# Quarter-array products in the triangular inverse of the gated delta rule

## The reference, cut to what matters

```
decay = exp(where(i >= j, gc[i] - gc[j], -inf))
lmat  = where(i > j, (k*beta) @ k.T * decay, 0)
tmat  = inverse(lmat + I)                        # unit lower triangular
u     = tmat @ (v * beta);  w = tmat @ (k * beta * exp(gc))
v_new = u - w @ s
o     = q_in @ s + (q @ k.T * decay) @ v_new
s     = s * exp(g_last) + k_out.T @ v_new
```

## Time and the profile before

| | |
|---|---|
| median of 3 runs (lowest, highest) | 3918.93 us (3916.99, 3925.47) |
| the profiled execution's time | 3921.35 us |
| its span, from first to last instruction | 3919.6 us |
| TensorE matmuls | 3528.7 us (90% of the span), 31266 instructions |
| VectorE | 1900.4 us (48%) |
| GpSimd | 1192.2 us (30%) |
| ScalarE | 1067.7 us (27%) |
| chain that ended last | PE 82%, ACT 6%, DVE 6%, issue 4%, DMA 1% |

### The profile page before, as it was taken

One profiled execution on the slowest core, in us unless ns is written; L12 is line 12 of the kernel. 1 busy time (PEld: TensorE's weight loads), 2 busy tenths in 40 slices (PEclk: granted clock), 3 DMA queues, 4 the chain that ended last, 5 costly groups with the idle time before them and its releaser, 6 DMA issues.

```text
span 3919.6 us, 74126 instructions
## 1 busy us (share of the span) xinstructions
PE 3528.7 (90%) x31266; PEld 3368.8 (86%) x31266; DVE 1900.4 (48%) x2402; ACT 1067.7 (27%) x1495; POOL 1192.2 (30%) x562
## 2 busy tenths in 40 slices
PE   8998787799999999989997876777699999999979
PEld 7997787799999999989996445777599999999979
DVE  1563554375454454655412225545447544544564
ACT  2365232242111111241013334222324111111142
POOL 2332532353333333333332000000064333333323
PEclk9999999899999999999998998998899999999989
DMA  3111000221111111112221016121121111111111
GB/s 126 57 52 52 1 0 24 83 65 49 43 43 43 43 43 43 49 56 84 91 72 47 1 43 214 36 43 35 65 99 51 43 43 43 43 43 43 43 44 70
DMA packets 106406, 212.49 MB, mean 54 GB/s; under 512 B 58560, under 2 KB 59840, under 8 KB 105600
## 3 DMA queue, kind: packets, MB, share of 16 engines
q1 hardware_dynamic: 94832, 168.65, 13.8%
q10 hardware_dynamic: 11408, 41.34, 2.7%
HBM read 172.73 MB, written 37.23 MB: 54 GB/s over the span
## 4 chain that ended last, share of the span: by engine, by line
PE 82%; ACT 6%; DVE 6%; issue 4%; DMA 1%; POOL 0%; ACTq 0%; DVEq 0%; SPq 0%; PEldq 0%; POOLq 0%
PE PS L727 56%; PE PS L744 8%; PE PS L1333 6%; PE PS L992 4%; PE PS L1298 1%; PE PS L1397 1%; ACT XH L1654 1%; ACT Y L1655 1%; PE PS L1356 1%; PE PS L1276 1%; DVE XL L2193 1%; PE PS L1273 1%; PE PS L758 0%; PE PS L1258 0%; PE PS L920 0%
## 5 line engine op out<-in xcount | busy, mean ns | idle before, releaser
L727 PE MATMUL PS<-XH,WHI 128*128 128x274 f32 x4320 | 1254.7, 290 | 11.4 <-ACT RN L1549 6.3
L727 PE MATMUL PS<-XL,WHI 128*128 128x274 f32 x4320 | 1254.0, 290 | 0.0
L727 PE MATMUL PS<-XH,WLO 128*128 128x274 f32 x4320 | 1252.0, 290 | 0.0
L843 POOL TENSOR_TENSOR WHI<-RAW,EPS 128x1024 fp32r<-128x1024 f32 x234 | 454.4, 1942 | 2452.5 <-PE PS L727 1417.4
L727 PEld LDWEIGHTS PS<-XH,WHI 128*128 128x128 f32 x4320 | 817.6, 189 | 14.4 <-issue 8.0
L727 PEld LDWEIGHTS PS<-XL,WHI 128*128 128x128 f32 x4320 | 819.2, 190 | 0.0
L727 PEld LDWEIGHTS PS<-XH,WLO 128*128 128x128 f32 x4320 | 818.5, 189 | 0.0
L846 POOL TENSOR_TENSOR WLO<-RAW,WHI 128x1024 fp32r<-128x1024 f32 x234 | 605.0, 2586 | 18.4
L727 PE MATMUL PS<-HH,WHI 128*128 128x274 f32 x1280 | 372.0, 291 | 0.0
L727 PE MATMUL PS<-HH,WLO 128*128 128x274 f32 x1280 | 370.4, 289 | 0.0
L727 PE MATMUL PS<-HL,WHI 128*128 128x274 f32 x1280 | 369.5, 289 | 0.0
(11 more groups left out here) (440 smaller groups left out, 5676.4 us busy)
## 6 DMA issues: line engine op xcount, KB each, us to landing
RAW<-in_units SPq DMA_DIRECT2D x234, 512.0 KB, 3.5
prepared_rows<-PREP SPq DMA_DIRECT2D x8, 1096.0 KB, 5.4
CIN<-prepared_rows SPq DMA_DIRECT2D x17, 512.0 KB, 4.5
c_rows<-DX ACTq DMA_DIRECT2D x14, 548.0 KB, 2.8
RKV<-c_rows SPq DMA_DIRECT2D x4, 1644.0 KB, 11.0
X<-in_x SPq DMA_DIRECT2D x8, 548.0 KB, 9.0
XR<-in_x ACTq DMA_DIRECT2D x8, 548.0 KB, 11.8
bonus_gate_rows<-BG SPq DMA_DIRECT2D x4, 1096.0 KB, 5.0
```

What stands on the lines that cost most here:

```text
L727: last = nc.tensor.matmul(PS[:, 4 * slot + b, 0:width], wt[:, ring, w], r[:, k, b * width:(b + 1) * width], start=n == 0, stop=n == 3 * nk ...
L843: nc.gpsimd.tensor_tensor(WHI[:, s, :], RAW[:, s, :], ZERO.to_broadcast([128, 1024]), ALU.add)\
```

## The change

The matrix of 128 tokens has two diagonal blocks of 64 and one block of 64x64 below them. Levels 0 to 5 never leave the diagonal blocks. After the change they work on buffers of 128 partitions x 4 heads x 64 columns (`TA_B`, `TT_B`, `WW_B`, `LM_B`, `DB_B`), the upper block in the upper half of the partitions and the lower one in the lower half, and every product of them is a `c_heads` group of 16 matmuls of 64x64. The masks of the levels are `BLOCK_LEVEL`, copied once before the loop. VectorE makes the diagonal blocks of `DB` in two halves and, as a new event `below`, the block below them; the transposing product now waits for `below`. Level 6 becomes two products on one quarter, of which one reads the block below in `DB`. Its negated result goes into a quarter of `TT`, and ScalarE copies the two diagonal blocks into `TT` (event `packed`), for which `carry1` now waits. The last quarter of `TT` is set to zero once. `m6` goes away.

```diff
+        BLOCK_LEVEL = at("BLOCK_LEVEL", [128, 6, 64], spare)
+        TT_B = [at("TT_B%d" % p, [128, 4, 64], spare + 1536 + 1024 * p) for p in range(2)]
+        TA_B = [at("TA_B%d" % p, [128, 4, 64], SETS[p][7]) for p in range(2)]
+        DB_B = [at("DB_B%d" % p, [128, 4, 64], SETS[p][7] + 1024) for p in range(2)]
+        WW_B = [at("WW_B%d" % p, [128, 4, 64], SETS[p][9]) for p in range(2)]
+        LM_B = [at("LM_B%d" % p, [128, 4, 64], SETS[p][9] + 1024) for p in range(2)]
...
 # GpSimd
-                    nc.gpsimd.tensor_tensor(LM[p][:, :, :], DB[p][:, :, :], heads_of(level_mask(l)), ALU.mult).then_inc(s, 1)
+                    nc.gpsimd.tensor_tensor(LM_B[p][:, :, :], DB_B[p][:, :, :], pairs_of(BLOCK_LEVEL[:, l, :]), ALU.mult)\
+                        .then_inc(s, 1)
...
-                elif name[0] == "w" and name != "w6":
+                elif name[0] == "w" and int(name[1]) < 5:
...
 # TensorE
                 elif name == "blocks":
-                    pe.wait_ge(gdn_dve[p], G_DVE.at(j, "m0"))
-                    turned(b + 1, LM[p]).then_inc(s, 1)
+                    pe.wait_ge(gdn_dve[p], G_DVE.at(j, "below"))
+                    tiled()
+                    c_heads(stacked(b + 1), LM_B[p], PAIR_ID).then_inc(s, 1)
...
-                    pe.wait_ge(gdn_pool[p], G_POOL.at(j, "m%d" % l))
-                    by_head(b + 1, LM[p], TT[p]).then_inc(s, 1)
+                    if l < 6:
+                        pe.wait_ge(gdn_pool[p], G_POOL.at(j, "m%d" % l))
+                        tiled()
+                        c_heads(stacked(b + 1), LM_B[p], TT_B[p]).then_inc(s, 1)
+                    else:
+
+                        tiled()
+                        for m in range(4):
+                            last = nc.tensor.matmul(stacked(b + 1)[half(0), m, :], DB[p][half(1), m, half(0)], TT_B[p][half(1), m, :],
+                                                    start=True, stop=True)
+                        last.then_inc(s, 1)
...
-                    by_head(b + 2, TA[p], WW[p]).then_inc(s, 1)
+                    tiled()
                     if l < 6:
-                        by_head(b + 3, WW[p], TA[p]).then_inc(s, 1)
+                        c_heads(stacked(b + 2), TA_B[p], WW_B[p]).then_inc(s, 1)
+                        c_heads(stacked(b + 3), WW_B[p], TA_B[p]).then_inc(s, 1)
                     else:
-
+                        for m in range(4):
+                            last = nc.tensor.matmul(stacked(b + 2)[half(0), m, :], TA_B[p][half(0), m, :], WW_B[p][half(0), m, :],
+                                                    start=True, stop=True)
+                        last.then_inc(s, 1)
...
                     pe.wait_ge(gdn_dve[p], G_DVE.at(j, "r"))
+                    pe.wait_ge(gdn_act[p], G_ACT.at(j, "packed"))
                     by_head(b + 1, TT[p], RR[p]).then_inc(s, 1)
...
 # ScalarE
-                    nc.scalar.activation(WW[p][:, :, :], per_head(b + 1), ACT.Copy).then_inc(s, 1)
+                    rows_of = slice(0, 128) if name != "w6" else half(0)
+                    nc.scalar.activation(WW_B[p][rows_of, :, :], stacked(b + 1)[rows_of, :, :], ACT.Copy).then_inc(s, 1)
+                    if name == "w6":
+
+                        act.wait_ge(gdn_dve[p], G_DVE.at(j, "tt5"))
+                        for h in range(2):
+                            last = nc.scalar.activation(TT[p][half(h), :, half(h)], TT_B[p][half(h), :, :], ACT.Copy)
+                        last.then_inc(s, 1)
...
 # VectorE, before the loop
+            for h in range(2):
+                nc.vector.tensor_copy(BLOCK_LEVEL[half(h), :, :],
+                                      small("level", 6 * 128).rearrange("p (l c) -> p l c", l=6)[half(h), :, half(h)])
+            dve.wait_ge(norm_done, 10)
+            for p in range(2):
+                nc.vector.memset(TT[p][half(1), :, half(0)], 0.0)
...
 # VectorE, in the loop
-                    nc.vector.tensor_tensor(DB[p][:, :, :], per_head(b + 1), DB[p][:, :, :], ALU.mult).then_inc(s, 1)
+                    for h in range(2):
+                        last = nc.vector.tensor_tensor(DB_B[p][half(h), :, :], per_head(b + 1)[half(h), :, half(h)],
+                                                       DB[p][half(h), :, half(h)], ALU.mult)
+                    last.then_inc(s, 1)
...
-                    nc.vector.tensor_tensor(LM[p][:, :, :], DB[p][:, :, :], heads_of(level_mask(0)), ALU.mult).then_inc(s, 1)
+                    nc.vector.tensor_tensor(LM_B[p][:, :, :], DB_B[p][:, :, :], pairs_of(BLOCK_LEVEL[:, 0, :]), ALU.mult)\
+                        .then_inc(s, 1)
...
-                    nc.vector.tensor_tensor(TA[p][:, :, :], heads_of(IDENT), LM[p][:, :, :], ALU.subtract).then_inc(s, 1)
+                    nc.vector.tensor_tensor(TA_B[p][:, :, :], pairs_of(PAIR_ID), LM_B[p][:, :, :], ALU.subtract).then_inc(s, 1)
+                    nc.vector.tensor_tensor(DB[p][half(1), :, half(0)], per_head(b + 1)[half(1), :, half(0)],
+                                            DB[p][half(1), :, half(0)], ALU.mult).then_inc(s, 1)
                     dve.wait_ge(gdn_pe[p], G_PE.at(j, "m_turned"))
-                    nc.vector.tensor_tensor(TT[p][:, :, :], heads_of(IDENT), per_head(b + 1), ALU.subtract).then_inc(s, 1)
+                    nc.vector.tensor_tensor(TT_B[p][:, :, :], pairs_of(PAIR_ID), stacked(b + 1), ALU.subtract).then_inc(s, 1)
...
-                    nc.vector.tensor_tensor(TT[p][:, :, :], TT[p][:, :, :], per_head(b + 2), ALU.subtract).then_inc(s, 1)
                     if name != "t6":
+                        nc.vector.tensor_tensor(TT_B[p][:, :, :], TT_B[p][:, :, :], stacked(b + 2), ALU.subtract).then_inc(s, 1)
...
+                        nc.vector.tensor_tensor(TA_B[p][:, :, :], TA_B[p][:, :, :], stacked(b + 3), ALU.subtract).then_inc(s, 1)
                     else:
+                        nc.vector.tensor_scalar(TT[p][half(0), :, half(1)], stacked(b + 2)[half(0), :, :], -1.0, None, ALU.mult)\
+                            .then_inc(s, 1)
```

More of the change, by code:

```diff
@@ L314, in build @@
         KT, QT, VT, DA, DB, EG, LM = [pair(x, n) for n, x in enumerate(("KT", "QT", "VT", "DA", "DB", "EG", "LM"))]
-        TA, TT, WW, VB, KO, RR, VN = [pair(x, 7 + n) for n, x in enumerate(("TA", "TT", "WW", "VB", "KO", "RR", "VN"))]
+        TT, VB, KO, RR, VN = [pair(x, n) for x, n in (("TT", 8), ("VB", 10), ("KO", 11), ("RR", 12), ("VN", 13))]
+        spare = 12 * TILE + 6 * SET
+        BLOCK_LEVEL = at("BLOCK_LEVEL", [128, 6, 64], spare)
[4 more added lines that the diff above has]
+        LM_B = [at("LM_B%d" % p, [128, 4, 64], SETS[p][9] + 1024) for p in range(2)]
         SP, SS = at("SP", [128, 4, 128], AR + 16 * TILE + 14 * SET), at("SS", [128, 4, 128], AR + 16 * TILE + 15 * SET)
@@ L503, in before @@
                 return i * self.count + 1
-        def level_mask(l):
-            return small("level", 128, 128 * l)
         def heads_of(x):
@@ L594, in build @@
                            *[x + str(l) for l in range(1, 7) for x in ("w", "tt", "ta")][:-1], "ks", "v_new", "o", "s")
-        G_DVE = ChunkStages("decayed", "diff", "lower", "m0", "ta0", "t0", "qk",
+        G_DVE = ChunkStages("decayed", "diff", "lower", "m0", "ta0", "below", "t0", "qk",
                             *[x + str(l) for l in range(1, 7) for x in ("tt", "ta")][:-1], "r", "s")
-        G_ACT = ChunkStages("staged", "exps", "ko", "vb", *["w%d" % l for l in range(1, 7)], "v_new", "out")
-        G_POOL = ChunkStages("upper", "m1", "q_in", *["m%d" % l for l in range(2, 7)])
+        G_ACT = ChunkStages("staged", "exps", "ko", "vb", *["w%d" % l for l in range(1, 7)], "packed", "v_new", "out")
+        G_POOL = ChunkStages("upper", "m1", "q_in", *["m%d" % l for l in range(2, 6)])
         C_PE = ChunkStages("vt", "l", "lt", "kg", "bg",
@@ L988, in _, with c_heads, tiled @@
             pe.wait_ge(norm_root, 8)
+            def c_heads(out, lhs, rhs, more=()):
+                terms = [(lhs, rhs)] + list(more)
+                for m in range(4):
+                    for n, (l, r) in enumerate(terms):
+                        for h in range(2):
+                            x = r[half(h), :] if len(r.shape) == 2 else r[half(h), m, :]
+                            last = nc.tensor.matmul(out[half(h), m, :], l[half(h), m, :], x,
+                                                    start=n == 0, stop=n == len(terms) - 1)
+                return last
+            def tiled():
+                pe.sem_inc(c_turn, 1)
             def by_head(bank, lhs, rhs, start=True, stop=True):
@@ L1031, in g_step @@
                     pe.wait_ge(gdn_act[p], G_ACT.at(j, "w%d" % l))
-                    by_head(b + 2, TA[p], WW[p]).then_inc(s, 1)
+                    tiled()
                     if l < 6:
-                        by_head(b + 3, WW[p], TA[p]).then_inc(s, 1)
-                    else:
+                        c_heads(stacked(b + 2), TA_B[p], WW_B[p]).then_inc(s, 1)
```

(6 more changed lines are left out.)

1 line of the change is left out of this document (removed).

## The result

| | median us | runs | profiled span us | clock |
|---|---|---|---|---|
| before | 3920.58 | 7 | 3919.6 | 0.957 |
| after | 3904.36 (3898.26 to 3910.39) | 7 | 3902.6 | 0.951 |

The ratio is 0.9959, 95% interval 0.9948 to 0.9970: 16 us faster, where 38 were forecast, and outside the range on its slow side.

A forecast was written before the change was run, and what follows sets the result against it. TensorE's queue in the gated delta stage was taken as the bound; blocks of 26.5 us for 30.94 give 31 over seven, plus 4.1 and 4.0 at the ends, less 1.2 set-up: 37.9 off 3918.93, so 3881 us, range 3867 to 3900.

The forecast's parts named there:

- The rival on code: Delta loop's longer code no longer stays in the chip: two back edges at 2.6 us plus low clock, 9 us, 3890; chance 0.25.
- Quarter products: Delta block on TensorE: sixteen 64x64 matmuls take 0.47 us for 0.89 in fifteen products, 6.3 us less a block.
- the Trainium skill's rule on banks: Row tiles cannot access one bank together: quarter groups near 0.93 us; the rival of halves not running together, 3935, chance 0.04.
- Changes of shape: TensorE alternating whole-array and quarter products, twelve times a delta block: 0.20 us for ten of them, 2.0 us a block.
- the upper bound of 0.42 for the marker: Price of a shape change if the marker before each quarter group (`tiled`) costs as much again as the 0.21 us change.
- `t3`: TensorE's wait in a delta block for ScalarE's copy: 0.8 us, against 0.88 before.
- row product: TensorE's wait in a delta block for VectorE's subtraction and full-width product: 1.4 us, against 1.57 before.
- `blocks`: TensorE's wait in a delta block for VectorE's half product: 2.4 us, against 2.1 before.
- `carry1`: TensorE's wait in a delta block for RR: 1.2 us, against 1.01 before.
- The lower halves: VectorE operations starting in another quadrant wait for earlier ones by the skill: 0.09 us later, some 0.3 us a block.
- Clock: TensorE's time at 1.2 GHz in a delta block: 2.5 to 4.7 us, costing 1.5 us, between 1.1 and 2.7.
- Ends: Delta stage outside its seven blocks: 4.1 us gained before the first update, 4.0 in the last tile, 1.2 lost to set-up.

The follow-up runs named there:

- before + 66: Kernel before plus 66 semaphore increments in TensorE's queue, where it idles ahead of the feed-forward part; 3930.99 us, ratio 1.0035.
- after + 192: Changed kernel plus 192 semaphore increments in TensorE's queue, where it idles ahead of the feed-forward part; 3894.19 us, ratio 0.9941.
- the doubled increments: Changed kernel with each of a block's 13 increments ahead of the delta stage's quarter groups (`tiled`) issued twice; 3878.03 us, ratio 0.9893.
- after + 32: Changed kernel plus 32 semaphore increments in TensorE's queue, where it idles ahead of the feed-forward part; 3866.48 us, ratio 0.9874.
- the runs without and with the moved mask: Changed kernel, 32 increments, `below` before `ta0`: GpSimd's upper mask cut to one of 128 columns, 3855.84 us; or made to wait for VectorE's `lower`, 3855.60 us.
- after + 14: Changed kernel plus 14 semaphore increments in TensorE's queue, where it idles ahead of the feed-forward part; 3864.49 us, ratio 0.9856.
- before + 98: Kernel before plus 98 semaphore increments in TensorE's queue, where it idles ahead of the feed-forward part; 3898.42 us, ratio 0.9942.

## Why the prediction was wrong

**The step that failed** is in its first part: "Everything before and after the stage is untouched, and behind it ScalarE squares the stage's output at once, so what the stage gains reaches the end." No instruction behind the stage was changed, but all were moved. The trace counts 3748 TensorE instructions for 2402 from the branch ahead of the delta loop to the first one behind it, with the loop's body once (1425 for some 877): 1346 more, 1320 loads and matmuls and 26 others. That is five pieces of 256 and 66. So the loop's start came to stand 12 instructions in front of a piece's end instead of 78, and each of six edges paid 2.6 us a second time where it had paid 1: 10 of the loop's 13.4 us; its way to the first edge took 1.8 more. That the place of the loop is the cause of the 13.4 is shown from both sides, by before + 66 (344.4 us) and after + 192 (332.7 us).

**The rival on code** saw the mechanism and its price (2.6 to 3.2 us an edge) in the earlier trace rows and asked about it only for the loop that grew. That loop held: no packet of instructions for TensorE moves from 491 to 607 us, in which both of its back edges lie (492.9 and 547.5), and its body of 1425 instructions by the trace fits where 1798 do not. The question was right, the loop wrong: code behind the change had to be asked about too, most of all a loop that already stopped.

**The rest of the loss.** Of the 31.7 us of lead, 7.7 go between the feed-forward loop's start and the first RWKV update. In attention it loses 2.8 us against before + 66, 1.9 of them in one stretch of low clock that the kernel before doesn't have: fourteen loads take 3.06 us where the earlier trace rows have 1.64. Timeline and window there:

```profile
2202.56 3.06 PEld L1333 LDWEIGHTS PS<-VTOK,PTB 128*128 128x128 f32 x14 [1.70 <-DVE PTB L2514]
```
```profile
2202.50:2205.90 3.40, 3.34 (x15) 3.34 (x16) 0.20 (x2) 0.72 (x2) 0.00 (x0) 0.50 0.00 0
```

VectorE's reduction ahead of it started 0.3 us later than in before + 66, and TensorE's wait, 1.43 us there, was 1.70. Why that start is later, no run settles. Nearly all of the rest is lost in the 100 us before the first RWKV update, and it is not stand-still: over the 244 us before that update (237 in before + 66) TensorE is idle 0.9 us longer. From the first feed-forward product on, 6.8 us more are at the lower clock than in before + 66, two stretches of 3.4, which at 0.4 to 0.5 us lost for each explain 3 to 4 of the 7 us. The others stay open. From the feed-forward loop's start to the first RWKV update the six runs with a changed stage and the RWKV loop 2 to 20 instructions into a piece need 1578 us, the three with it where the changed kernel has it or 64 instructions before that 1581 to 1582; with the old stage it is 1574, 1575 with 66 increments and 1578 with 98; with the doubled increments it is 1580. At the place of the changed kernel the two stages differ by 7 us, at the place of after + 32 by nothing. So it goes with stage and placement together.

**The terms of the stage,** in order. *Quarter products* 0.47 us apart (500.40 and 500.87), as forecast; the eight passes on one quarter alone take 0.54 from the first load to the end of the last, as the sixteen do. In two quarters they write one bank together, so the Trainium skill's rule on banks in TensorEngine Tiling was rightly set aside by the rows. *Changes of shape* 0.14 to 0.17 for 0.20; the upper bound of 0.42 for the marker is excluded by its doubling. Timeline:

```profile
500.87 0.55 PEld L1002 LDWEIGHTS PS<-TA_B,WW_B 64*64 64x64 f32 x16
...
501.48 0.42 PEld L1018 LDWEIGHTS PS<-SMALL,VT 128*128 128x128 f32 x4
...
502.07 0.54 PEld L1002 LDWEIGHTS PS<-TT_B,LM_B 64*64 64x64 f32 x16 [0.17 <-issue]
```

*Waits:* `t3` 0.68 for 0.8, row product 1.25 for 1.4, `blocks` 3.15 in some tiles and 2.48 in others for 2.4 (3.05 to 3.14 in all of after + 32), `carry1` 1.63 for 1.2. Both that were too small are VectorE beside GpSimd, which the runs without and with the moved mask show for DB*BETA: DB*BETA takes 1.34 us where it took 0.88 in the interval that the sum started from, RR+VB 1.01 for 0.69. The halved masks moved GpSimd's full ones against VectorE's steps, and the sum kept the old durations. The lower halves:

```profile
503.41 0.86 DVE L2142 TENSOR_TENSOR DB_B<-PS,DB 64x256 f32<-64x256 f32 x2
```

Two operations of 0.43 us in 0.86, so the second started only when the first had ended. That agrees with the rule cited from the Trainium skill, VectorE: DVE Perf Modes; it costs 0.1 us here. *Clock:* 0.90 in this profile, about a fifth of a block at the lower level, some 2.2 us for 1.5. The block of 26.5 came out at 27.3 here, 26.9 and 26.8 in the runs with 32 and 14 increments, whose clock was 0.92: half of the miss goes with the clock. *Ends:* first update 2.8 us sooner with the set-up in it (2.9 forecast), last tile 3.4 for 4.0; its levels stand 2.5 us apart as forecast. So the stage is 31.6 us shorter here and 35 in those two runs, for 37.9. With the RWKV loop in about the same place before and after, the change gives 34 us at the front of a piece (after + 14 against before + 98), about 30 where the changed kernel has it (ratios 0.9959 and 1.0035) and 28 where the kernel before has it (after + 192 is 21.7 us faster, and its increments cost 6). All three lie within the forecast's range of 21 to 54, and all below its 38.

## What to carry to other kernels

Code added to a long program moves every loop behind it. For each loop whose body doesn't stay on the chip, look for stops on "issue" at its back edge, count from there to the next stop inside a product, and forecast both for the new position; a few harmless instructions in an idle stretch ahead of the loop may be worth more than the change under study, here 33 to 40 us against 28 to 34. Count the added instructions in the trace, not from calls in the source: how many a call makes differs with its form. And compare two versions of a kernel at the same placement, or the difference says little of the edit. Where two engines share a stretch, ask which operation the slowed one is doing, and let it be one that nobody waits for.

## What the runs showed of the hardware

- TensorE's code comes in pieces of 256 instructions, each asked for when the one before it is entered, and takes about 3 us to arrive, by the stops. A loop that spans seven pieces ran with no fetch; one of eight, of 1798 instructions, with none at two of three edges if the branch stood 9 or 27 instructions into the eighth, at one of two if it stood 60, at none if it stood 184 to 250 (five kernels). The pattern of threes and twos is not explained.
- The loop moved within a piece by just the 66 instructions by which 1346 exceed five pieces. A transposition of a head is one pass, two instructions, and a block of four heads 8; the quarter products that replace it are 32.
- A stop costs more than itself: in after + 32 the RWKV iterations behind an edge that ran through had a granted clock of 1.00, the one behind a stop of 4.8 us had 0.88 and took 6.8 us longer.
- An operation on VectorE that reads and writes only SBUF, 0.68 us alone, took 1.34 beside a GpSimd multiplication; those that read PSUM (0.43 for the half product) did not slow beside one.
